# Expert layer: where the fourteen later choices of experts stand among the groups of rows

## The reference

```python
def peer_ffn(hn, w_pq, sub_keys, u_tab, v_tab):
    ...
    q = (xt @ w_pq).reshape(T, PEER_HEADS, 2, PEER_D_KEY // 2)
    s = jnp.einsum('thpd,hpkd->thpk', q, sub_keys).astype(jnp.float32)
    top_s, top_i = lax.top_k(s, K)
    cand = top_s[:, :, 0, :, None] + top_s[:, :, 1, None, :]
    best_s, best_c = lax.top_k(cand.reshape(T, PEER_HEADS, K * K), K)
    ia = jnp.take_along_axis(top_i[:, :, 0], best_c // K, axis=-1)
    ib = jnp.take_along_axis(top_i[:, :, 1], best_c % K, axis=-1)
    expert = ia * PEER_N_KEYS + ib
    gate = jax.nn.softmax(best_s, axis=-1)
    ...
        a = jnp.einsum('td,ted->te', xb, u_tab[eb])
        hidden = gb.astype(xb.dtype) * jax.nn.gelu(a)
        return jnp.einsum('te,ted->td', hidden, v_tab[eb])
```

## Time and profile before

| what | us |
|---|---|
| median of 3 runs (lowest, highest) | 3143.16 (3134.68, 3144.44) |
| the profiled execution | 3140.97 |
| its span, first to last instruction | 3139.1 |
| first product of a u row | 1888.82 |
| first product of group 5 | 2157.54 |
| busy: PE / DVE / ACT / POOL | 2751.3 / 2113.9 / 1148.5 / 985.0 |

### The profile page before, as it was taken

The page is one execution under the profiler, slowest core; times in us unless marked ns, Lnnn a source line. Parts: engine busy times, 40 slices in busy tenths (PEclk is TensorE's granted clock), DMA queues, the critical chain, the costliest instruction groups (busy, mean ns, idle before and its releaser), DMA issues.

```text
span 3139.1 us, 34650 instructions
## 1 busy us (share of the span) xinstructions
PE 2751.3 (88%) x12196; PEld 1993.0 (63%) x12196; DVE 2113.9 (67%) x2872; ACT 1148.5 (37%) x1982; POOL 985.0 (31%) x566
## 2 busy tenths in 40 slices
PE   8999999999999999999989994666767777679997
PEld 7888788888887888999778892222223343235433
DVE  5587565555564555445555569888788888779877
ACT  5455555555553335445655541000002330034000
POOL 0011000000000000000000007877778877778864
PEclk9999999999999999989999996888898888978999
DMA  6444445555554554443334449999999999999997
GB/s 250 155 161 148 174 179 187 189 192 189 188 187 170 187 187 171 162 170 126 134 138 171 163 175 398 403 416 415 410 419 410 418 410 405 408 397 369 409 403 305
DMA packets 123586, 827.89 MB, mean 264 GB/s; under 512 B 22167, under 2 KB 22183, under 8 KB 23855
## 3 DMA queue, kind: packets, MB, share of 16 engines
q0 software_dynamic: 79392, 510.36, 40.1%
q1 hardware_dynamic: 43920, 313.73, 27.6%
q10 hardware_dynamic: 144, 2.10, 0.2%
HBM read 892.00 MB, written 4.22 MB: 285 GB/s over the span
## 4 chain that ended last, share of the span: by engine, by line
PE 20%; POOL 13%; DVE 9%; DMA 8%; issue 4%; ACT 2%; DVEq 0%; ACTq 0%
POOL rows L1296 13%; PE ps L598 11%; DMA rows<-peer_u,arena 5%; PE ps L1203 3%; DVE arena L2402 3%; PE ps L1214 2%; DMA rows<-peer_v 2%; DMA rows<-peer_v,arena 1%; PE ps L1194 1%; DVE arena L209 1%; DVE arena L202 0%; ACT arena L1762 0%; DVE arena L203 0%; DVE arena L206 0%; DVE arena L199 0%
## 5 line engine op out<-in xcount | busy, mean ns | idle before, releaser
L503 DVE SCALAR_TENSOR_TENSOR WL<-ring,PA,WH 128x512 fp32r<-128x512 f32 x896 | 632.5, 752 | 473.9 <-ACT WH L486 458.6
L1214 PE MATMUL ps<-rows,rstd 128*128 128x512 f32 x1164 | 638.8, 703 | 289.6 <-DMA rows<-peer_v,arena 203.6
L2402 DVE CUSTOM_DVE_ANT_0 arena<-rows,arena 128x2048 f32<-128x2048 f32 x256 | 586.9, 2293 | 140.9 <-DMA rows<-peer_u,arena 111.7
L1214 PEld LDWEIGHTS ps<-rows,rstd 128*128 128x128 f32 x1164 | 250.0, 224 | 664.9 <-issue 383.0
L1296 POOL DMA_INDIRECT rows<-peer_v,arena x256 | 483.2, 1888 | 197.2 <-DVE arena L2402 72.9
L485 ACT ACTIVATE WH<-ring,PA 128x512 fp32r<-128x512 f32 x448 | 324.0, 723 | 547.1 <-PE ps L598 395.9
L1296 POOL DMA_INDIRECT rows<-peer_u,arena x256 | 449.4, 1756 | 167.2 <-DVE WL L503 82.2
L598 PE MATMUL ps<-WH,HH 128*128 128x512 f32 x1120 | 443.3, 396 | 8.6 <-DVE WL L503 6.2
L598 PE MATMUL ps<-WH,HL 128*128 128x512 f32 x1120 | 438.6, 392 | 0.0
L598 PE MATMUL ps<-WL,HH 128*128 128x512 f32 x1120 | 438.5, 391 | 0.0
L598 PE MATMUL ps<-HH,WH 128*128 128x256 f32 x1088 | 312.3, 287 | 21.1 <-DVE WL L503 21.1
(11 more groups left out here) (361 smaller groups left out, 3574.5 us busy)
## 6 DMA issues: line engine op xcount, KB each, us to landing
ring<-stream SPq DMA_DIRECT2D x292, 1024.0 KB, 4.8
rows<-peer_v POOLq DMA_DIRECT2D x32, 1024.0 KB, 15.6
rows<-peer_u,arena POOLq DMA_INDIRECT x256, 14.1
rows<-peer_v,arena POOLq DMA_INDIRECT x256, 14.3
arena<-xT SPq DMA_DIRECT2D x4, 512.0 KB, 8.9
bias_rows<-bias_scratch POOLq DMA_DIRECT2D x1, 2048.0 KB, 12.6
arena<-xT ACTq DMA_DIRECT2D x1, 2048.0 KB, 10.8
arena<-memT POOLq DMA_DIRECT2D x1, 2048.0 KB, 9.1
```

The source lines that it names most:

```text
L503: ins = nc.vector.scalar_tensor_tensor(out=half_tile(WL, u)[:, s], in0=raw_half(u)[:, s], scalar=gain[d], in1=half_tile(WH, u).bitcast(f32 ...
L1214: last = mm(ps[:, 4 * tt + q, :], DIAG[:, k % DIAGS, :], rows[:, SLOTS[n % ROWS], q * CH:(q + 1) * CH], start=n == mine[0], stop=n == ends[q])
L2402: ins = V.tensor_tensor_reduce(out=JUNK, in0=rows[:, SLOTS[n % ROWS], :], in1=HN[:, tt, :], scale=1.0, scalar=0.0, op0=ALU.mult, op1=ALU.a ...
```

## The change

The table `CHOOSE_AT` gives, for a pair of group and row, the group to be chosen behind that u row. It puts three choices into each of groups 0 to 3 (behind rows 2, 7 and 12) and two into group 4 (behind rows 2 and 7), which are the choices of groups 2 to 15. Groups 5 to 15 have none. `gate` of each follows on ScalarE three rows behind its choice.

```diff
+CHOOSE_AT = {(k // 3, 2 + 5 * (k % 3)): EARLY + k for k in range(GROUPS - EARLY)}
...
-                if tab == "u" and j == 12 and 0 < g <= GROUPS - EARLY:
-                    gate(g + EARLY - 1)
+                if tab == "u" and (g, j - 3) in CHOOSE_AT:
+                    gate(CHOOSE_AT[g, j - 3])
...
-                    if j == 2 and 0 < g <= GROUPS - EARLY:
+                    if (g, j) in CHOOSE_AT:
                         dve.wait_ge(sem("rows_dve"), done)
-                        choose(g + EARLY - 1)
+                        choose(CHOOSE_AT[g, j])
```

## The result

The changed kernel takes 3209.23 us (median of 4 runs, 3206.81 to 3211.09) against 3143.8 us before (the three runs of the table above and one more). The ratio is 1.0214, 95% interval 1.0193 to 1.0235: slower by 67 us by the ratio (61 to 74), where 3208 was forecast. Of two executions of one kernel, the first products alone can start 5 us apart (1883.5 to 1888.8 us over the traces in which nothing ahead of them was moved), so single differences of a few microseconds in the end say little; starts counted from a run's own first product say more. The span of its profiled execution is 3205.0 us, 65.9 more than before.

The account below looks back on a forecast made before the run. VectorE was taken to bound groups 0 and 1, transfers the groups from 2 on. The profiled 3140.97 us plus 66.3 (72.4 later at group 5, 6 given back, 0 after) gave 3207.3, stated as 3208; range 3185 to 3236.

Parts of the forecast that it names:

- unit prices: VectorE's time for each piece: 2.445 us a product row, 0.73 a `poly`, 1.06 a `finish`, 9.83 a choice.
- step 1: Groups 0 to 4, now with 14 choices: 341.1 us of VectorE work, no waits, group 5 72.4 us later.
- Step 2: Group 5: 6 us come back from rows already in the ring, first wait at row 8, 66.3 us remain.
- Step 3: Groups 6 to 15 and what follows: the ten choices that left groups 5 to 14 return nothing, 0 us.
- Rival 1: Groups 5 to 14: GpSimd's issues become the bound, 61.1 us a group for 57.9, total 3240 us; chance 0.14.
- Rival 2: Groups 5 to 14 shorten from 57.9 to 55.9 us, giving back 20 us, total 3188 us; chance 0.12.
- rival 3: Early groups: 12-row ring hides VectorE's lag, 3141 us; last sentence: it takes up no extra 28 us (3185); chance 0.03.

Follow-up runs that it names:

- the late triple: Changed kernel with one choice in groups 1 to 4, three in group 5, none in 6 and 7, one in 8 to 14: 3147.64 against 3140.84 us before.

## Why the prediction was right

The unit prices and the sum of step 1 held: 2229.9 us forecast for group 5, 2230.23 measured, and in three more arrangements the work up to the group behind the last choices came within 0.2 to 1.0 us of the sum, counted from each run's own first product. VectorE did not wait for a transfer before 2246.96 us, so the ring and GpSimd kept up with it, as step 1 said. That it is VectorE's excess and not GpSimd's stops is shown by the same 14 choices costing 16, 32, 54, 67 and 126 us.

Step 2 was right in kind, and what it took as given back a little large. The first wait came at row 6 of group 5 and not at row 8; row 8 of group 5 came at 2253.76 (forecast 2252.2), row 11 at 2265.51 (2263.8), so 68.0 us of delay stood there and not 66.3, and 68.9 at group 6. The end was 65.9 us later all the same: the part behind the groups took 343.5 us, 2.8 less than before. From the last product of a u row to the end of the span it is 350.7 us before and 347.5 after, and 347.8 to 349.8 in the nine other traces, those with choices in the late groups and those without mixed: spread between executions. So the mechanism was right, but that the end fits to half a microsecond is luck, two small errors that cancel.

Step 3 was right: 521.3 us with and without nine choices, the work gone replaced by waiting. That the two agree to a tenth is luck: the same stretch takes 519.6 to 527.8 us in the four traces with eight or nine choices in it, and 517.7 to 521.3 in the four with none, so a gain of a few microseconds is not excluded, one of 20 is. The share of the DMA engines was named as a sign of step 1: a DMA share of 0.82 near 340 GB/s in groups 1 to 3 came out as 0.84, 0.90, 0.90 and 316 to 343 GB/s: the bytes a second fit, the share is higher, so it is the poorer measure of the two. GpSimd was to be without long waits in the late groups, and was not quite: over groups 6 to 14 it waited 33.1 us in 18 pieces, up to 7.7 us, for slots that TensorE frees, where before it had waited 44.4 us for VectorE and 7.1 for TensorE. The DMA share stayed at 1.01 all the same. And the page of the earlier trace rows shows the DMA engines full in 15 of the last 16 slices, not in all.

Rival 1 did not come: from issue to landing a u row took 10.4 us in group 5 and 16.6 in group 6 (medians of the DMA issues below, of groups 5 and 6 after), and 22.6 in group 14, so GpSimd was ahead of the transfers and drew further ahead. Its mechanism is there on a small scale, in the group behind a full ring, where the late triple shows it.

```profile
rows<-peer_u,arena POOLq DMA_INDIRECT x16, 10.4
```

```profile
rows<-peer_u,arena POOLq DMA_INDIRECT x18, 16.6
```

Rival 2, with its 20 us, is refuted by those stretches, rival 3 by group 5's start. The weakest point of the text on record is rival 3's last sentence: the ring does take up a lag, about half of 13.6 us in the late triple, where the groups behind it are free of choices; it could not here, because three groups of excess followed one another.

## What to carry to other kernels

Before work that uses no data of a stream is gathered at its start, compare, stretch by stretch, the engine's own work with the transfers' time: here moving it out of stretches that had slack gained nothing, and where stretches without slack followed one another nearly all of the excess was paid. Slack can't be saved up: the ring of 12 rows carried a lag of 4 us into the next group for nothing and took back about half of one of 13.6. The sum of one engine's instructions over a stretch that it bounds is worth doing to the microsecond; here it held to 1 us in sums of 341 to 464.

## What the runs showed of the hardware

An issue of an indirect transfer takes GpSimd 0.99 us at its shortest and 2.14 behind products of VectorE; the one group behind a full ring in the late triple, with such issues, ran at 373 GB/s where the next did 420. The Trainium skill, GPSIMD Engine Reference, section "Key points", says that GpSimd shares its SBUF interfaces with VectorE and contends with VectorE instructions that have two SBUF inputs; the 2.14 us beside 0.99 agree with it. In the changed kernel it cost little: without choices VectorE waits for rows and so frees GpSimd by itself. I had not expected the queue of transfers to grow there, to 16.6 us from issue to landing in group 6 and 22.6 in group 14, with no choice to let GpSimd catch up.
